# Half of the tokens of a PEER layer through all experts densely on TensorE, the other half still gathered

## The chip, the cores and the metric

The kernel runs on one core of a Trainium2 chip. The metric is the device time of one execution in microseconds, as the median of several runs; lower is better. A core has TensorE (PE, matmuls into PSUM, with weight loads listed as PEld), VectorE (DVE), ScalarE (ACT), GpSimd (POOL) and SyncE (SP), and 16 DMA engines that all queues share. SP issues plain transfers, POOL the indirect ones (gathers of rows by index).

## What is computed

One encoder layer over 512 tokens of width 1024, in float32: a token-mixing part (spatial gating and retention), then PEER, a retrieval over 16,384 experts that each are one row of `u` and one of `v`. Every token picks 16 experts in each of 8 heads:

```python
q = (h @ w_q).reshape(b, s, PEER_HEADS, 2, PEER_KEY_DIM)
scores = jnp.einsum('bshpd,hpnd->bshpn', q, sub_keys)     # 2 x 128 keys per head
top_s, top_i = lax.top_k(scores, 16)                      # of each half
cand_s = top_s[..., 0, :, None] + top_s[..., 1, None, :]  # 256 candidates
cand_i = top_i[..., 0, :, None] * 128 + top_i[..., 1, None, :]
best_s, best_pos = lax.top_k(cand_s.reshape(...), 16)
gates = softmax(best_s)                                   # over the 16
act = gelu(einsum('td,ted->te', x, u_tab[idx]))
out = einsum('te,ted->td', gates * act, v_tab[idx])
x <- LayerNorm(2**0.25 * h + out)
```

An expert's number is 128 i + j, from the two halves' keys i and j.

## The kernel before, in words

The tokens lie on the 128 partitions in four tiles (NT = 4). The token-mixing part runs first and is the same in both kernels up to the output projection ("out") and the first layer norm. For the rest, a *unit* is one head of one tile of tokens: 32 units of 16 experts for 128 tokens. For each unit and each of its 16 choices, POOL gathers 128 rows of `u` (one per token, 4 KB each, 512 KB in all) and later 128 rows of `v`, into rings of RING = 8 buffers each (`urow`, `vrow` in `big`). Every gather is one indirect DMA (L427, `block_of_gathers`), the two tables in turn.

- DVE, per unit (`unit`): 8 dot products of `u` rows with the tokens (`products`, L863, which also reads the sum out), the sum of an earlier unit out of PSUM (`add_unit`, L856), the choice of the *next* unit's experts (`choose`, L799 to L848: top 16 of 128 twice, top 16 of 256, indices), 8 more products, and the weights (L875).
- ACT, per unit: the exponentials, the GELU of the 16 dots, and 16 diagonal matrices of the weights (`diagonals`, L504).
- PE, per unit: `add_rows` (L1011), per expert two matmuls of 512 columns, diagonal matrix times the 128 `v` rows, that sum up in PSUM.
- Only the first units are written out, between the heads' queries (L969, `query`) and key scores (L1152, `keys`) on PE; from unit 8 (PE, ACT, DVE) or 2 (POOL) the engines run loops.

`static_jobs` writes the order of PE's and ACT's work by hand and gives each job its PSUM bank. One float32 matmul shows as two MATMUL records in the trace.

## Time and profile before

| | us |
|---|---|
| median of 3 runs | 1776.52 |
| lowest, highest run | 1762.88, 1776.70 |
| span of the profiled execution, first to last instruction | 1921.2 |
| PE busy in it | 1402.8 |
| DVE busy | 1125.5 |
| POOL busy | 1186.6 |

For the profiled execution only the span is known; what lies around its first and last instruction isn't in the page. Busy shares are means over the front part (about 244 us here) and the expert part, which have different limits. "issue" is the name for an engine's idle time in which it waited for nothing that the profile shows.

### The profile page before, as it was taken

Reading aid. Unit: us, or ns where it says so; the run is one execution under the profiler, and the core shown is the slowest. Engines: PE = TensorE matmul, PEld = TensorE weight load, DVE = VectorE, ACT = ScalarE, POOL = GpSimd, SP = SyncE. Lnnn points to the kernel's source line nnn. Section 1 sums busy time; section 2 is a strip of 40 time slices with the busy share of each in tenths; the row PEclk is TensorE's granted clock in tenths of the full one; section 3 lists DMA queues with packets and bytes.
Section 4 is the critical chain, followed back from the end, with each engine's and each line's share of the span. In section 5 each row is a group of like instructions: output and inputs, shape, how many; then the busy total and the mean of one; then the engine's idle time right before and its main releaser. Section 6 shows DMA issues by size and latency. Waiting matters only on the chain.

```text
span 1921.2 us, 14461 instructions
## 1 busy us (share of the span) xinstructions
PE 1402.8 (73%) x3572; PEld 633.5 (33%) x3572; DVE 1125.5 (59%) x2765; ACT 344.1 (18%) x792; POOL 1186.6 (62%) x1061
## 2 busy tenths in 40 slices
PE   8999798889899865566665666576657666675666
PEld 6777444334345322222222222122212222222222
DVE  5663578555655557555655655655546565546565
ACT  4230112222112211111111111111111111111110
POOL 2341177666676765677766666676767666667764
PEclk9999898999999998899988998898989889998989
DMA  6214299988999998788988889798979888888987
GB/s 230 84 71 148 91 354 332 383 323 324 343 360 341 357 347 299 289 322 326 340 318 307 317 334 353 261 368 314 357 277 355 304 307 318 310 334 310 367 294 264
DMA packets 173537, 577.87 MB, mean 301 GB/s; under 512 B 17712, under 2 KB 30512, under 8 KB 173488
## 3 DMA queue, kind: packets, MB, share of 16 engines
q0 software_dynamic: 147456, 536.94, 75.6%
q1 hardware_dynamic: 26032, 40.38, 6.0%
q8 instruction: 19, 0.31, 0.1%
q14 instruction: 30, 0.25, 0.0%
HBM read 575.15 MB, written 2.10 MB: 300 GB/s over the span
## 4 chain that ended last, share of the span: by engine, by line
PE 22%; DVE 20%; issue 20%; DMA 15%; POOL 14%; DVEq 6%; another core or an unknown queue 2%; ACT 1%; POOLq 0%; SPq 0%; ACTq 0%
POOL big L427 14%; DMA big<-in_peer_u_dram,idxu 11%; PE ps L1011 7%; DVE big L863 7%; PE ps L969 5%; PE ps L986 5%; DMA big<-in_peer_v_dram,idxv 4%; DVE y L856 1%; DVE mixT L802 1%; DVEq L818 1%; DVE topi L801 1%; DVE pick L846 1%; DVEq L800 1%; DVE top L804 1%
## 5 line engine op out<-in xcount | busy, mean ns | idle before, releaser
L1011 PE MATMUL ps<-big,diag 128*128 128x512 f32 x1968 | 1001.4, 644 | 472.6 <-DMA big<-in_peer_v_dram,idxv 219.5
L863 DVE CUSTOM_DVE_ANT_0 big<-big,mixT 128x1024 f32<-128x1024 f32 x480 | 571.6, 1224 | 417.0 <-DMA big<-in_peer_u_dram,idxu 399.9
L427 POOL DMA_INDIRECT big<-in_peer_v_dram,idxv x496 | 557.9, 1125 | 306.1 <-issue 145.0
L1011 PEld LDWEIGHTS ps<-big,diag 128*128 128x128 f32 x1968 | 364.6, 201 | 1100.9 <-issue 787.8
L427 POOL DMA_INDIRECT big<-in_peer_u_dram,idxu x512 | 548.0, 1070 | 264.3 <-issue 144.5
L504 ACT ACTIVATE diag<-ident,wgt 128x128 f32<-128x128 f32 x508 | 159.6, 389 | 500.0 <-PE ps L1011 370.3
L334 POOL TENSOR_TENSOR weight_parts<-big,weight_parts 128x1024 fp32r<-128x1024 f32 x20 | 49.0, 2474 | 84.6 <-ACT weight_parts L486 84.5
L969 PE MATMUL ps<-xT,qkT 128*128 128x512 f32 (+1 forms) x256 | 98.9, 539 | 1.1 <-ACTq L571 1.1
L986 PE MATMUL ps<-weight_parts,x_hi 128*128 128x512 f32 x320 | 82.8, 404 | 0.8 <-ACT weight_parts L486 0.8
L969 PEld LDWEIGHTS ps<-xT,qkT 128*128 128x128 f32 x256 | 48.6, 190 | 50.1 <-issue 35.3
L986 PEld LDWEIGHTS ps<-weight_parts,x_hi 128*128 128x128 f32 x320 | 59.8, 191 | 14.8 <-ACT weight_parts L486 2.4
L496 ACT ACTIVATE gel<-dots 128x16 f32<-128x16 f32 x32 | 6.9, 216 | 309.6 <-DVE dots L863 309.5
L490 ACT ACTIVATE eg<-best,negmax 128x16 f32<-128x16 f32 x33 | 10.1, 307 | 279.3 <-DVE negmax L832 192.6
L486 ACT ACTIVATE mixT<-ps 128x512 f32<-128x512 f32 (+1 forms) x20 | 11.1, 555 | 234.4 <-PE ps L969 118.1
L863 DVE DVE_READ_ACCUMULATOR2_ANT dots<- 128x1 f32 x512 | 41.9, 82 | 0.0
L490 ACT ACT_TABLE_LOAD x32 | 41.1, 1283 | 0.7
L496 ACT ACT_TABLE_LOAD x32 | 41.1, 1283 | 0.6
L986 PE MATMUL ps<-weight_parts,x_lo 128*128 128x512 f32 x160 | 40.2, 394 | 0.0
L863 DVE CUSTOM_DVE_ANT_0 big<-big,y 128x1024 f32<-128x1024 f32 x32 | 37.3, 1222 | 3.6 <-DMA big<-in_peer_u_dram,idxu 3.4
L856 DVE TENSOR_TENSOR y<-y,ps 128x1024 f32 (+1 forms) x32 | 38.9, 1216 | 0.2
L804 DVE MAX8 best<-mixT 128x8 f32<-128x256 f32 x30 | 12.8, 428 | 42.7 <-issue 41.6
L986 PEld LDWEIGHTS ps<-weight_parts,x_lo 128*128 128x128 f32 x160 | 30.6, 192 | 6.7
(179 smaller groups left out, 947.5 us busy)
## 6 DMA issues: line engine op xcount, KB each, us to landing
big<-in_w_in_dram SPq DMA_DIRECT2D x24, 512.0 KB, 5.8
qkT<-in_peer_w_q_dram SPq DMA_DIRECT2D x12, 1024.0 KB
big<-in_peer_u_dram,idxu POOLq DMA_INDIRECT x512
big<-in_peer_v_dram,idxv POOLq DMA_INDIRECT x496
xh<-in_x_dram SPq DMA_DIRECT2D x8, 512.0 KB, 10.7
big<-in_w_out_dram SPq DMA_DIRECT2D x2, 2048.0 KB, 10.7
out_dram<-y SPq DMA_DIRECT2D x8, 256.0 KB
lnp<-in_ln_w_dram SPq DMA_DIRECT2D x2, 512.0 KB, 6.9
```

The source lines that it names most:

```text
L334: return engine.tensor_tensor(w_lo(g)[:, ks, :], w_full(g)[:, ks, :], w_hi(g)[:, ks, :].bitcast(f32), ALU.subtract)
L427: nc.gpsimd.indirect_dma_start(row[e % RING], None, table, bass.IndirectOffsetOnAxis(ap=index[:, e:e + 1], axis=0)).then_inc(signal[e % RI ...
L490: A.activation(eg[:, k, :], best[:, k, :], ACT.Exp, bias=negmax[:, k:k + 1], accum_out=esum[:, k:k + 1]).then_inc(s_exp, 1)
L496: A.activation(gel[:, k, :], dots[:, k, :], ACT.Gelu).then_inc(s_gel, 1)
L504: A.activation(diag[:, e % NDIAG, :], ident[:], ACT.Copy, scale=wgt[:, k, e:e + 1]).then_inc(s_diag, 1)
L800: fence()
L804: V.max(values[:, 8:16], spare)
L856: V.tensor_tensor(yt, yt, acc[k], ALU.add).then_inc(s_yadd, 1)
L863: V.tensor_tensor_reduce(out=urow[e % RING], in0=urow[e % RING], in1=hcur, scale=1.0, scalar=0.0, op0=ALU.mult, op1=ALU.add, accum_out=dot ...
L969: last = T.matmul(dst, lhs(i), rhs(i), start=(i == 0), stop=(i == n - 1))
L986: last = T.matmul(dst, *((a, b_) if x_left else (b_, a)), start=(n == 0 and k == 0), stop=(n == 2 and k == KC - 1))
L1011: last = T.matmul(acc[k][:, half * 512:(half + 1) * 512], diag[:, e % NDIAG, :], ring[e % RING][:, half * 512:(half + 1) * 512], start=(e ...
```

## The change

Tiles 0 and 1 (GATHERED = 2; 16 units) stay gathered. Tiles 2 and 3 (DENSE = 256 tokens) go through all 16,384 experts:

- the host writes `u` a second time, as 128 blocks in a transposed layout (`u_blocks`); SP streams the 128 `u` blocks and the 128 `v` blocks of 128 experts, 512 KB each, through a ring of four buffers (`load_block`), in two rounds: 64 `u` blocks, 64 `v` blocks, twice.
- "act" on PE: per `u` block 8 matmuls of 256 columns, and ACT's GELU of two blocks at a time into `X` (128 experts x 256 tokens per block i).
- "gates": DVE builds for each token two one-hot matrices over its 128 choices, one of key j (128 wide) and one of key i (64 wide in a round) times the gate (`onehots`); PE multiplies them (64 columns per token), which gives the token's 128 x 64 gate matrix; DVE multiplies it into `X` (`dense_weights`). `gate_round` does 32 groups of 8 tokens per round.
- "expert" on PE: per `v` block 4 matmuls of 512 columns, weights `X`, into the PSUM banks that the gathered sums used.
- the gathered half no longer uses PE and the diagonals: DVE adds each gathered `v` row times its weight to the tokens' sum (`add_rows`, L897 of the changed kernel), two units behind the products.
- DVE chooses for the 16 dense heads of two tiles at a stroke, 5, 5 and 6 of them in the first three units. The gate rounds stand behind unit 3 and unit 11.
- all loops are written out; buffers are laid over one another in `pool_mem`; POOL takes a `u` row and a `v` row in turn, each waiting for one slot of its ring instead of four.
- queries of tiles 0/1 and 2/3 are separate matmuls, since the transposed tokens lie in two halves; the first chooses and the norms of tiles 1 to 3 change places.

```diff
+GATHERED = 2
+GUNITS = GATHERED * PH
+DENSE = (NT - GATHERED) * P
+HALF = NK // 2
+DRING = 4
+FILL = list(range(16, HALF)) + list(range(16))
...
+    for r in range(2):
+        for n in range(HALF // 2):
+            add("act", r, n, by="act")
+            for u in after.get((r, n), ()):
+                jobs.append(("gelu", (u,), None))
+        if r == 0:
+            jobs.append(("gates", (), None))
+            add("selT", 0, by="act")
+            add("selT", 1, by="act")
+        for n in range(DENSE // 8):
+            add("gate", r, n, by="dve")
+        for u in range(3, 8) if r == 0 else range(12, GUNITS):
+            jobs.append(("gelu", (u,), None))
+        for n in range(HALF):
+            jobs.append(("expert", (r, n), None))
...
+            def load_block(b):
+                r, n = divmod(b, 2 * HALF)
+                if b == 1:
+                    sp.wait_ge(s_sc0, TILE0)
+                elif b == 2:
+                    sp.wait_ge(s_wqd, TILE0 + PH)
+                elif b >= DRING:
+                    sp.wait_ge(s_blkd, b - DRING + 1)
...
+            def gather_u(n):
+                u, e = divmod(n, TOPK)
+                if e == 0:
+                    pool.wait_ge(s_idx, u + 1)
+                if n >= RING:
+                    pool.wait_ge(s_dot, n - RING + 1)
...
+            def gather_v(n):
+                if n >= RING:
+                    pool.wait_ge(s_vadd, n - RING + 1)
...
+            lag = 2 * TOPK
+            for n in range(GUNITS * TOPK + lag):
+                if n < GUNITS * TOPK:
+                    gather_u(n)
+                if n >= lag:
+                    gather_v(n - lag)
...
+            def add_rows(u, e0, e1):
+                for e in range(e0, e1):
+                    n = TOPK * u + e
+                    dve.wait_ge(s_v[n % RING], 16 * (1 + n // RING))
+                    V.scalar_tensor_tensor(acc_rows[t], vrow[n % RING], wgt[:, u, e:e + 1], acc_rows[t],
+                                           ALU.mult, ALU.add).then_inc(s_vadd, 1)
                     fence()
...
+                V.tensor_tensor(ohi[:, q], spread(0, HALF),
+                                iota[:, r * HALF:(r + 1) * HALF].unsqueeze(1).broadcast_to([P, 4, HALF]),
+                                ALU.is_equal)
+                V.tensor_tensor(ohj[:, q], spread(1, NK), iota[:].unsqueeze(1).broadcast_to([P, 4, NK]),
+                                ALU.is_equal)
+                fence()
+                V.tensor_tensor(ohi[:, q], ohi[:, q], spread(2, HALF), ALU.mult)
+                fence().then_inc(s_oh, 1)
...
+            chooses = [5, 5, 6]
+            for u in range(GUNITS):
+                products(u, 0, TOPK // 2)
+                if u >= 2:
+                    weights(u - 2)
+                    add_rows(u - 2, 0, TOPK // 2)
+                if u + 2 < GUNITS:
+                    choose_gathered(u + 2)
+                if u < len(chooses):
+                    for n in range(sum(chooses[:u]), sum(chooses[:u + 1])):
+                        choose_dense(n)
...
+                products(u, TOPK // 2, TOPK)
...
+                if u >= 2:
+                    add_rows(u - 2, TOPK // 2, TOPK)
+                if u == 3:
+                    gate_round(0)
+                if u == 11:
+                    gate_round(1)
...
+            for u in range(GUNITS - 2, GUNITS):
+                weights(u)
+                add_rows(u, 0, TOPK)
+            finish(acc_rows[1]).then_inc(s_ln2, 1)
             fence()
+            dve.wait_ge(s_vdone, 1)
+            for a in range(2):
...
+                rows_v = block_of(r, HALF + i)
+                for a in range(2):
+                    for half in range(2):
+                        last = T.matmul(acc[a][:, half * 512:(half + 1) * 512], X[:, i, a * P:(a + 1) * P],
+                                        rows_v[:, half * 512:(half + 1) * 512], start=(r == 0 and i == 0),
+                                        stop=(r == 1 and i == HALF - 1))
...
+                        last = product(bank[:, q * DENSE:(q + 1) * DENSE], lambda k: cols[:, k, :],
+                                       lambda k: hT[:, 1, k, :], KC)
+                        T.drain().then_inc(s_blkd, 1)
```

PE, behind the last norms of the first part. In the kernel before, queries (L969), key scores (L1152) and the expert rows of the first units (L1011, `S` and `big` hold the `v` rows, `diag` the diagonals) alternate:

```order
L1119 MATMUL ps<-ident,xh 128x128 x8
L969 MATMUL ps<-xT,qkT 128x512 x8
L1011 MATMUL ps<-big,diag 128x512 x10
L969 MATMUL ps<-xT,qkT 128x512 x8
L1152 MATMUL ps<-keysT,mixT 128x128 x8
L1011 MATMUL ps<-big,diag 128x512 x22
```

In the changed kernel the last query and keys are followed by the blocks, one row per ring buffer (`wr`, `y` and two in `xT`), with 256 columns a matmul, and, further on, by the transposes of the choices and the gate matmuls of the first round:

```order
L1012 MATMUL ps<-xT,pool_mem 128x256 x8
L1197 MATMUL ps<-pool_mem 128x128 x9
L1012 MATMUL ps<-xT,wr 128x256 x8
L1012 MATMUL ps<-xT,y 128x256 x8
L1012 MATMUL ps<-xT 128x256 x16
```

```order
L1209 MATMUL ps<-ident,sel 128x128
L1210 MATMUL ps<-ident,sel 128x128
L1211 MATMUL ps<-ident,gated 128x128
L1219 MATMUL ps<-ohi,y 128x64 x256
```

PE no longer has any row of a gathered unit; its whole expert part hangs on the blocks and on the one-hots.

DVE, the end of one unit and the start of the next. Before (unit 2 and 3; `ISA` is a product or its read-out):

```order
L863 ISA big,dots<-big,mixT 128x1024
L863 ISA dots 128x1
L872 RECIPROCAL rsum<-esum 128x1
L875 SCALAR_TENSOR_TENSOR wgt<-gel,rsum,eg 128x16
L863 ISA big,dots<-big,mixT 128x1024
L863 ISA dots 128x1
```

In the changed kernel, at unit 3's end, 8 rows are added (`y` is the sum), and the gate round follows, one group of 8 tokens being two sets of three rows and one product into `X` (in `pool_mem`):

```order
L877 ISA big,dots<-big,xh 128x1024
L877 ISA dots 128x1
L897 SCALAR_TENSOR_TENSOR y<-big,wgt,y 128x1024 x8
L914 TENSOR_TENSOR ohi<-selT,iota 128x256
L917 TENSOR_TENSOR y<-selT,iota 128x512
L920 TENSOR_TENSOR ohi<-ohi,selT 128x256
L914 TENSOR_TENSOR ohi<-selT,iota 128x256
L917 TENSOR_TENSOR y<-selT,iota 128x512
L920 TENSOR_TENSOR ohi<-ohi,selT 128x256
L927 TENSOR_TENSOR pool_mem<-ps,pool_mem 128x64x8
```

Every unit of the gathered half now has two such groups of 8 added rows on DVE, which PE did before.

## Rows read from the trace of the kernel before

**Rows 1.** The page: span, busy time, chain of waits, queue of gathers.
```profile
span 1921.2 us, 14461 instructions
PE 1402.8 (73%) x3572; PEld 633.5 (33%) x3572; DVE 1125.5 (59%) x2765; ACT 344.1 (18%) x792; POOL 1186.6 (62%) x1061
...
q0 software_dynamic: 147456, 536.94, 75.6%
...
PE 22%; DVE 20%; issue 20%; DMA 15%; POOL 14%; DVEq 6%; another core or an unknown queue 2%; ACT 1%; POOLq 0%; SPq 0%; ACTq 0%
```

**Rows 2.** Groups by line and shape: busy us, mean ns | idle before, by releaser.
```profile
L1011 PE MATMUL ps<-big,diag 128*128 128x512 f32 x1968 | 1001.4, 644 | 472.6 <-DMA big<-in_peer_v_dram,idxv 219.5 <-ACT diag L504 212.0 <-issue 40.9
L863 DVE CUSTOM_DVE_ANT_0 big<-big,mixT 128x1024 f32<-128x1024 f32 x480 | 571.6, 1224 | 417.0 <-DMA big<-in_peer_u_dram,idxu 399.9 <-issue 16.1
L427 POOL DMA_INDIRECT big<-in_peer_v_dram,idxv x496 | 557.9, 1125 | 306.1 <-issue 145.0 <-PE ps L1011 96.8 <-DVE idxu L848 42.0
...
L804 DVE MAX8 best<-mixT 128x8 f32<-128x256 f32 x30 | 12.8, 428 | 42.7 <-issue 41.6
...
L834 DVE CAST posf<-posab 128x32 f32<-128x32 uint32 x33 | 6.4, 193 | 25.9 <-issue 23.9
...
L743 DVE TENSOR_TENSOR S<-ps,S 128x512 f32<-128x512 f32 x4 | 2.7, 685 | 0.1
```

**Rows 3.** Stretches of 5 us: busy per engine, PEclk, DMA share, GB/s.
```profile
330.00:335.00 5.00, 5.00 (x15) 2.19 (x14) 5.00 (x10) 0.00 (x0) 4.39 (x3) 1.00 1.03 413
1030.00:1035.00 5.00, 3.83 (x9) 1.25 (x8) 1.23 (x6) 0.00 (x0) 3.78 (x5) 1.00 1.04 416
1040.00:1045.00 5.00, 1.92 (x4) 0.61 (x4) 4.64 (x10) 0.00 (x0) 1.33 (x1) 1.00 0.18 30
1045.00:1050.00 5.00, 0.00 (x0) 0.00 (x0) 5.00 (x9) 0.00 (x0) 2.84 (x2) 0.66 0.44 143
```

**Rows 4.** PE in order of time: start us, us, line, shape, records.
```profile
217.23 5.35 PE L1127 MATMUL ps<-xT,qkT 128*128 128x128 f32 x32
...
259.43 3.73 PE L1127 MATMUL ps<-xT,qkT 128*128 128x128 f32 x32
...
264.43 13.90 PE L969 MATMUL ps<-big,mixT 128*128 128x512 f32 x32
...
352.94 7.03 PE L969 MATMUL ps<-xT,qkT 128*128 128x512 f32 x16
```

**Rows 5.** DVE in order of time, one choose and the first products.
```profile
234.41 0.28 DVE L799 MAX8 top<-ropet 128x8 f32<-128x128 f32 x1
...
244.46 1.23 DVE L863 CUSTOM_DVE_ANT_0 big<-big,y 128x1024 f32<-128x1024 f32 x1
245.61 0.08 DVE L863 DVE_READ_ACCUMULATOR2_ANT dots<- 128x1 f32 x1
245.61 1.22 DVE L863 CUSTOM_DVE_ANT_0 big<-big,y 128x1024 f32<-128x1024 f32 x1
```

**Rows 6.** POOL in order of time; DVE's products run back to back until 268.3.
```profile
262.57 1.99 POOL L427 DMA_INDIRECT big<-in_peer_u_dram,idxu  x1 [0.30 <-issue]
...
269.45 0.94 POOL L427 DMA_INDIRECT S<-in_peer_v_dram,idxv  x1 [0.30 <-issue]
```

**Rows 7.** DVE in order of time: pairs of 256 elements, an added row, a norm.
```profile
231.62 0.76 DVE L839 TENSOR_TENSOR y<-posf,iota 128x256 f32<-128x256 f32 x2
232.45 0.76 DVE L844 TENSOR_TENSOR y<-y,topf 128x256 f32<-128x256 f32 x2
...
1910.29 1.28 DVE L957 SCALAR_TENSOR_TENSOR y<-big,wgt,y 128x1024 f32<-128x1024 f32 x1
1911.65 1.29 DVE L645 BATCH_NORM_STATS2 st<-y 128x6 f32<-128x512 f32 x2
...
1917.95 0.75 DVE L653 SCALAR_TENSOR_TENSOR y<-y,nw,lnp 128x512 f32<-128x512 f32 x1
```

**Rows 8.** The page's DMA issues: transfer, queue, count, KB each, us to landing.
```profile
big<-in_w_in_dram SPq DMA_DIRECT2D x24, 512.0 KB, 5.8
```

More of the change, by code:

```diff
@@ L147, in static_jobs @@
     for i, (kind, arg, by) in enumerate(jobs):
-        if kind in ("V", "split", "norm"):
+        if kind in ("split", "norm", "scale", "gelu", "gates", "expert"):
             placed.append((kind, arg, by, None, None))
@@ L499, in diagonals @@
-            def diagonals(u, k, e0=0, e1=TOPK, first=False):
-                for e in range(e0, e1):
-                    if (e % 4 == 0 or e == e0) and not (first and e < NDIAG):
-                        act.wait_ge(s_vexp, 16 * u + min(e - e % 4 + 4, e1) - NDIAG)
-                    A.activation(diag[:, e % NDIAG, :], ident[:], ACT.Copy,
-                                 scale=wgt[:, k, e:e + 1]).then_inc(s_diag, 1)
-            act.wait_ge(s_const, 4)
-            A.activation(gel[:, 0, 0:1], ident[:, 0:1], ACT.Gelu)
@@ L592, in _ @@
                     A.drain().then_inc(s_sc, 1)
[L594 to L604 removed]
+                elif kind == "act":
+                    r, n_ = arg
+                    i = FILL[2 * n_] if r == 0 else 2 * n_
+                    if i == 0 and r == 0:
+                        act.wait_ge(s_chosen, 2 * PH)
+                    if i == 48 and r == 0:
+                        act.wait_ge(s_h, 2 * NT)
+                    A.activation(X[:, i:i + 2, :], bank.rearrange("p (i n) -> p i n", i=2), ACT.Gelu
+                                 ).then_inc(free[b], 1)
+                    if n_ == HALF // 2 - 1:
+                        A.drain().then_inc(s_act, 1)
+                elif kind == "selT":
+                    a = arg[0]
+                    copy(selT[:, :, a * P:(a + 1) * P], bank4[:, 0:3, :]).then_inc(free[b], 1)
+                    A.drain().then_inc(s_selT, 1)
+            for t in range(GATHERED):
+                for half in range(2):
+                    act.wait_ge(s_ln2, 2 * t + half + 1)
+                    c = half * 512
+                    act.dma_start(out3[:, t, c:c + 512], acc_rows[t][:, c:c + 512]).then_inc(s_out, 16)
         @block.vector
@@ L827, in choose @@
                 fence()
[L828 removed]
+                top16(cand, values, pos[:], spare)
                 fence()
@@ new lines, in dense_weights, with gate_round @@
+            def dense_weights(r, n):
+                b, used_ = BANK["gate", r, n]
+                dve.wait_ge(full[b], used_ + 1)
+                x3 = X[:, :, 8 * n:8 * n + 8]
+                V.tensor_tensor(x3, ps[:, b, :].rearrange("p (t i) -> p i t", t=8), x3, ALU.mult).then_inc(free[b], 1)
+            def gate_round(r):
+                if r == 0:
+                    dve.wait_ge(s_selT, 2)
+                for n in range(DENSE // 8):
+                    onehots(r, n, 0)
+                    onehots(r, n, 1)
+                    if n == 1:
+                        dve.wait_ge(s_act, r + 1)
+                    if n:
+                        dense_weights(r, n - 1)
+                dense_weights(r, DENSE // 8 - 1)
+                fence().then_inc(s_wgtd, 1)
@@ L1162, in _ @@
                     T.drain().then_inc(s_scored, 1)
-            for u in range(EARLY, PH):
-                add_rows(u, u % 2)
-            with pe.Fori(PH // 2, UNITS // 2 - 1) as pair:
-                add_rows(2 * pair, 0)
-                add_rows(2 * pair + 1, 1)
-            add_rows(UNITS - 2, 0)
-            add_rows(UNITS - 1, 1, 0, LAST, end=LAST)
+            T.drain().then_inc(s_vdone, 1)
 _INS = ["x", "w_in", "sgu_ln_w", "sgu_ln_b", "sgu_w_s", "sgu_b", "ret_decay_fwd", "ret_decay_bwd", "ret_gn_w",
```

484 lines of the change are left out of this document (228 added, 256 removed).

## The prediction

> **What bounds the kernel now.** I read the page first: PE is busy 73% of 1921.2 us, POOL 62%, DVE 59%, and the chain of waits is spread over PE, DVE, POOL, DMA and "issue" with 14 to 22% each [rows 1]. No engine is the bound alone; a loop through several is. The groups by line say which: DVE's products sit idle 399.9 us for the gathered `u` rows, PE's expert rows 219.5 us for the `v` rows [rows 2]. So I looked at the transfers by stretch. While POOL issues without a pause they carry 413 to 416 GB/s at a share of 1.03 to 1.04; once per unit the rate falls to 30 and 143 GB/s, when DVE's choose had made POOL wait [rows 3]. POOL takes 0.94 + 0.30 = 1.24 us per gather [rows 6], and 0.524 MB per 1.24 us is 423 GB/s. The kernel before lives on this stream: 536.9 MB of gathers [rows 1], which alone need 1309 us at 410 GB/s.
>
> The profiled execution takes 1921.2 us and the runs 1776.5 us, 145 us less. DVE's choose shows idle time put down to "issue", 41.6 and 23.9 us in two of its groups alone [rows 2], and none where transfers are light: the choose at 234.41 runs through in 10.05 us [rows 5]. I take such gaps as the profiler's and work with durations without them. My sum is thus for a run without a profiler; set against the profiled execution's own 1921.2 us I would add about 60 to 110 us (22 of the 32 chooses under heavy transfers, at 3 to 5 us), giving a span of 1830 to 1880 for the changed kernel. A forecast made only in ratio to the span (1855 / 1921) would be 1715 us; I keep it inside the range.
>
> **The change part by part.** Removed: 16 of 32 units' gathers (268.4 MB), all diagonals, all L1011 matmuls. Added: 256 blocks of 0.524 MB (134.2 MB) from SP. Transfers of the expert part fall to 268.4 + 134.2 + 8.4 (the query weights) = 411 MB, 1002 us at 410 GB/s. That is room, if it can be used evenly.
>
> *PE.* 32 records of 512 columns take 13.90 us, 0.434 each; 32 of 128 columns 3.73 us, 0.117 each [rows 4]. An expert block is 8 records of 512: 3.47 us. An act block is 16 records of 256 columns: between 16 x 0.117 = 1.9 and 16 x 0.434 = 6.9 us; the two rows lie on a line through 0.22, so 3.5 us, and 0.1 for the drain. 128 blocks of each: 890 us. Queries: eight heads at 2 x 7.03 us, four of them three quarters of that, 98 us, and 112 records of 128 columns for the keys, 13 to 19 us at 0.117 to 0.167, in all some 115 us [rows 4]; they begin when tile 3 is normed.
>
> *DVE.* A product costs 245.61 - 244.46 = 1.15 us [rows 5]; 256 of them 294 us. An added row costs 1911.65 - 1910.29 = 1.36 us [rows 7]; 256: 348 us, which is new on DVE. Chooses: 32 x 10 = 320 us, as before. A gate group of 8 tokens: a pair of 256 elements with its fence takes 0.83 us [rows 7] and 512 elements from PSUM 0.685 us [rows 2], so 256 + 512 + fence 1.1, the second 256 0.5, twice, + 0.7 = 3.9 us; with hand-overs to PE 4.1. Lower bound 3.5 (all fences free), upper bound 3.9 + 8 x 2 x 0.167 = 6.6 (PE's records at the pace of its slower row, 5.35 us for 32 [rows 4], with nothing overlapped; the two sets of one-hot buffers speak for the low end). 32 groups: 131 us a round, and in it neither gathers nor blocks move but for full rings: this is the cost with nothing beside it, 262 us in two rounds.
>
> *The rings.* POOL's `v` gather needs a slot that only an added row frees. In the 8 products (9.2 us) it is stuck; then it owes DVE 16 gathers, 16 x 1.24 = 20 us, against 8 x 1.36 us of adding. Where DVE computes back to back, a gather takes up to 1.99 instead of 0.94 us [rows 6]; I add half of that, 0.5 us.
>
> The path, by stage:
> 1. To the start of the units: the last out group of tile 3 ends at 264.43 + 13.90 = 278.3 [rows 4]; two residuals and the norm (1911.65 to 1918.7, 7.1 us [rows 7]) take it to 287, choose(1) to 298.
> 2. Units 0 to 3: 64 products 73, 32 added rows 44, 4 chooses 40 and 16 dense ones at 9.8, 157, small ones 4: 317. Rows come late by some 5, 7, 12 and 12 us in the halves without a choose (20 us of POOL against 20 of DVE with a landing behind it): 353. This ends at 651. PE ends its queries at about 289 + 115 = 404 and the first 64 act blocks at 632, so it is hidden.
> 3. Gate round 0: 131, to 782.
> 4. Units 4 to 11. PE runs 64 expert and 64 act blocks, 450 us. DVE needs 16 x 1.15 + 16 x 1.36 + 10 + 1 = 51 us a unit. But PE's blocks take 0.524 MB per 3.5 us, 150 GB/s, and leave 260 of 410 for the gathers: 16.78 MB a unit is 64.5 us, plus 4 in which POOL is stuck, 69 us. Eight units: 6.5 in PE's 450 us, 1.5 at 51 + 4 to 5: 530; by bytes alone, 201 MB at 410, 491. I take 526, to 1308.
> 5. Gate round 1: 131, to 1439.
> 6. Units 12 to 15: 64 expert blocks, 222 us of PE; 3.2 units at 69 and 0.8 at 43, one norm 8: 255. Then 32 added rows, 44, plus 6 of waits, norm 8: 313, to 1752. PE is done at 1439 + 222 = 1661, hidden.
> 7. Two residuals and norms, 2 x 8.7, and the last store 2.5: 1772 us.
>
> Against 1776.5 that is no change. What halving the gathers gives, the gate rounds (262 us) and DVE's added rows (348 us) take back.
>
> The critical price is stage 4's rate. Of this the trace shows only one queue at a time at full load; two queues may carry less (370, which is 536.94 MB over 75.6% of the span [rows 1]) or more. At 370 the stages that hang on transfers give 1848, at 430 some 1735. I take 410, by the nearest rows. The Trainium skill (DMA: Bandwidth & Descriptors, "Where 436 GB/s comes from") puts the limit for loads from HBM at about 358 GB/s and the ports' at 435. The trace's 416 is above the first; by the second the sum would be an estimated 1727.
>
> **The rivals.**
> - *The stream hides it all* (faster). If the transfers of blocks and gathers don't hold each other up, stage 4 is PE's 450 and stage 6 DVE's 240 + 10: 1772 - 76 - 63 gives about 1635. For it: DVE and PE have slack in every stage. Against: it asks for 150 + 16.78 MB / 53 us = 467 GB/s, and no stretch shows over 416 [rows 3].
> - *The added rows lock POOL out* (slower). One mechanism: POOL's gather waits while DVE runs an op with two SBUF operands. Products show it: 1.99 us against 0.94, a pace of one gather per two products [rows 6]. Now all of the `v` slots come free during such ops. At a full 1.05 us more per gather issued in them, 16 gathers a unit lose 0.55 more each, 9 us, of which half is behind the stream: 4 to 5 us x 10 units in stages 2, 4, 6 adds about 45: 1818. It decides from about 0.8 us. Against: over the whole trace the mean gather is 1.125 [rows 2], so most slip between. The Trainium skill (SBUF — State Buffer, "SBUF: two separate sides") says a DVE op with two SBUF inputs and a GpSimd op that reads SBUF exclude each other for the whole instruction. It speaks against moving these sums from PE to DVE; rows 6 agree for products, and no run here shows it for an added row with its fence.
> - *PE is the bound of the gate rounds.* PE is busy half of the time there; if its clock falls to 1.2 GHz (the granted 0.66 of one stretch stands where PE was idle [rows 3]) and half of its work lies bare, a group takes 3.9 + 1.35 = 5.25 us, 37 more a round: 1846. It decides once PE's half group is longer than DVE's 1.6 us.
> - *The change doesn't do what it says*: blocks starve PE since the ring is four deep. 3 x 3.5 = 10.5 us of lead against a landing of 5.8 us for 512 KB [rows 8]; unlikely, and inside the last case.
>
> **How the numbers follow.** The forecast, 1772 with its own range 1735 to 1810, has a chance of 0.5; the hidden stream 0.2 (1635, with cases up to 1735); the lock 0.24 (1800 to 1840); the gate rounds on PE or starving 0.06 (1846). Within 1% of 1776.5 is 1759 to 1794, about what a measurement of this kernel can tell from no change. Of the forecast's half, 0.18 lies under, 0.20 within, 0.12 above. Faster by over 1%: 0.18 + 0.20 = 0.38, with 0.02 from the reading in ratio to the span 0.40; same 0.22; slower 0.12 + 0.24 + 0.06 less rounding, 0.38. The range for 8 in 10 reaches to 370 GB/s above and halfway to the hidden stream below: 1685 to 1850.
>
> **What would show it.** In the changed profile: act blocks in 3.5 us and expert blocks in 3.47; units 4 to 7 at 65 to 73 us with 390 GB/s or more and DVE's products and added rows waiting for gathers; gate rounds of 125 to 140 us with hardly a transfer; PE idle before gate round 1; the last PE matmul some 80 us before the end. Wrong would be: units 4 to 7 at 55 us (hidden stream), gathers of nearly 2 us in the added rows (lock), gate rounds over 150 us, or a span under 1780.

## The result and the profile after

The changed kernel takes 1868.06 us (median of 4 runs, 1864.51 to 1877.42) against 1772.6 us (4 runs) beside it: a ratio of 1.057, interval 1.052 to 1.063. It is 5.7% slower. On other occasions the kernel before itself takes 1917 to 1936 us (experiment 8), and the ratio there is 0.979. The forecast was 1772 in a range of 1685 to 1850, so the time lies 96 us over the forecast and 18 us outside the range.

The page of the changed kernel, against [rows 1]:

```profile
span 1862.6 us, 17614 instructions
...
PE 1535.9 (82%) x5898; PEld 1096.9 (59%) x5898; DVE 1305.2 (70%) x2763; ACT 170.5 (9%) x268; POOL 634.9 (34%) x548
...
PE   8999899999999805999999979789728999999500
...
DVE  5663367877683179888586576686688888755688
...
PEclk9999999999999955558999989899865559999855
DMA  6223334375954385006999989899983009999883
...
q0 software_dynamic: 73728, 268.47, 37.8%
```

POOL's busy time fell from 62% to 34% of the span and the gathers' bytes to half, as forecast. The time went into what the rows of digits show as holes. DVE falls to 1 and PE to 0 just ahead of the first gate round (slices 13 to 15); the transfers stand at 0 in both rounds; and PE's clock stands at 5 in both.

The span by the stages of the prediction, one stretch each (busy us per engine in the order PE, PEld, DVE, ACT, POOL, then PE's granted clock, the transfers' share and GB/s):

```profile
298.00:718.00 420.00, 335.00 (x1587) 276.44 (x1585) 277.94 (x839) 53.68 (x90) 103.68 (x92) 0.91 0.61 213
718.00:845.00 127.00, 116.69 (x512) 111.61 (x512) 111.96 (x224) 0.00 (x0) 9.23 (x9) 0.50 0.13 48
845.00:1397.00 552.00, 468.13 (x1537) 293.36 (x1536) 387.88 (x688) 42.67 (x72) 271.75 (x246) 0.93 0.92 355
1397.00:1527.00 130.00, 117.81 (x513) 112.18 (x514) 114.94 (x227) 0.00 (x0) 10.31 (x10) 0.50 0.13 51
1527.00:1841.00 314.00, 221.21 (x512) 97.49 (x510) 228.96 (x340) 9.77 (x16) 163.67 (x144) 0.85 0.90 343
```

| stage | forecast | measured |
|---|---|---|
| 2: units 0 to 3 | 353 | 420 |
| 3: gate round 0 | 131 | 127 |
| 4: units 4 to 11 | 526 | 552 |
| 5: gate round 1 | 131 | 130 |
| 6: units 12 to 15, last rows, norm | 313 | 314 |

Stages 2 and 4 are 67 + 26 = 93 us over, against 96 in all. The other three are right within 4 us.

Stage 2 is told by one row. DVE's waits, the two longest groups, and DVE and ACT in order of time around the second:

```profile
DVE big L877 <- DMA big<-in_peer_u_dram,idx: 242.9, 100, 5.1
DVE dsum L864 <- ACT gated L511: 69.2, 1, 69.2
```

```profile
576.01 1.22 DVE L877 CUSTOM_DVE_ANT_0 big<-big,xh 128x1024 f32<-128x1024 f32 x1
577.16 0.08 DVE L877 DVE_READ_ACCUMULATOR2_ANT dots<- 128x1 f32 x1
646.49 0.42 DVE L864 TENSOR_REDUCE dsum<-gated 128x16 f32<-128x256 f32 x1 [69.25 <-ACT gated L511]
```

```profile
636.30 0.60 ACT L587 ACTIVATE pool_mem<-ps 128x512 f32<-128x512 f32 x1 [7.15 <-PE ps L1012]
644.05 0.60 ACT L587 ACTIVATE pool_mem<-ps 128x512 f32<-128x512 f32 x1 [7.15 <-PE ps L1012]
644.74 1.28 ACT L511 ACT_TABLE_LOAD   x1
646.04 0.42 ACT L511 ACTIVATE gated<-gated 128x256 f32<-128x256 f32 x1
```

DVE has everything for the dense gates at 577 and needs one exponential of ACT. ACT is idle 7.15 us ahead of nearly every eviction (an eviction is the GELU that takes a pair of act blocks out of PSUM), but it works in the order of its program, and there the exponential (L511) stands behind the evictions of all 64 act blocks of round 0. So DVE waits for PE's whole act pass by way of ACT. Behind DVE's wait, on DVE, are the added rows of unit 2's second half and all of unit 3, none of which need a gate of the dense half.

### The profile page after: what moved, and what is told of

It is laid out like the page before. It is cut to its first block, busy times and chain, and to the rows that moved or that the text cites. A ratio compares the mean times of both kernels' runs of the same rounds, so it can differ in the third digit from the quotient of the medians.

```text
span 1862.6 us, 17614 instructions
## 1 busy us (share of the span) xinstructions
PE 1535.9 (82%) x5898; PEld 1096.9 (59%) x5898; DVE 1305.2 (70%) x2763; ACT 170.5 (9%) x268; POOL 634.9 (34%) x548
## 4 chain that ended last, share of the span: by engine, by line
PE 29%; DVE 23%; POOL 17%; DMA 16%; issue 8%; DVEq 5%; ACT 1%; SPq 0%; ACTq 0%
PE ps L1012 19%; DMA big<-in_peer_u_dram,idx 16%; POOL big L471 10%; POOL big L461 7%; DVE y L897 6%; PE ps L1029 5%; DVE big L877 3%; DVEq L919 3%; DVE ohi L920 3%; DVE pool_mem L927 2%; DVE y L917 2%; DVE ohi L914 1%; PE ps L1219 1%; PE ps L1197 1%; PE ps L1151 1%
## 5 line engine op out<-in xcount | busy, mean ns | idle before, releaser
L877 DVE CUSTOM_DVE_ANT_0 big<-big,xh 128x1024 f32<-128x1024 f32 x256 | 303.9, 1223 | 247.5 <-DMA big<-in_peer_u_dram,idx 242.9
L461 POOL DMA_INDIRECT big<-in_peer_u_dram,idx x256 | 275.8, 1077 | 587.2 <-DVE dots L877 457.5
L471 POOL DMA_INDIRECT big<-in_peer_v_dram,idx x256 | 298.1, 1164 | 466.2 <-DVE y L897 396.7
L897 DVE SCALAR_TENSOR_TENSOR y<-big,wgt,y 128x1024 f32<-128x1024 f32 x256 | 328.7, 1284 | 22.8 <-issue 1.0
L1219 PE MATMUL ps<-ohi,y 128*128 128x64 f32 x1024 | 233.6, 423 | 122.9 <-DVEq L921 122.9
L1219 PEld LDWEIGHTS ps<-ohi,y 128*128 128x128 f32 x1024 | 223.3, 330 | 133.7 <-issue 133.5
L1012 PE MATMUL ps<-xT 128*128 128x256 f32 x1024 | 243.5, 392 | 36.8 <-ACT pool_mem L587 26.7
L1012 PEld LDWEIGHTS ps<-xT 128*128 128x128 f32 x1024 | 193.8, 194 | 86.5 <-issue 33.6
L1064 PE MATMUL ps<-xT,pool_mem 128*128 128x512 f32 x512 | 224.9, 592 | 0.0
L1064 PEld LDWEIGHTS ps<-xT,pool_mem 128*128 128x128 f32 x512 | 97.3, 190 | 122.5 <-issue 122.5
L1012 PEld LDWEIGHTS ps<-xT,pool_mem 128*128 128x128 f32 x512 | 87.3, 193 | 12.1 <-issue 2.5
```

The source lines that it names most:

```text
L461: nc.gpsimd.indirect_dma_start(urow[n % RING], None, peer_u2, bass.IndirectOffsetOnAxis(ap=idx[:, u, e:e + 1], axis=0)).then_inc(s_u[n % R ...
L471: nc.gpsimd.indirect_dma_start(vrow[n % RING], None, peer_v2, bass.IndirectOffsetOnAxis(ap=idx[:, u, e:e + 1], axis=0)).then_inc(s_v[n % R ...
L877: V.tensor_tensor_reduce(out=urow[n % RING], in0=urow[n % RING], in1=xh[:, t * D:(t + 1) * D], scale=1.0, scalar=0.0, op0=ALU.mult, op1=AL ...
L897: V.scalar_tensor_tensor(acc_rows[t], vrow[n % RING], wgt[:, u, e:e + 1], acc_rows[t], ALU.mult, ALU.add).then_inc(s_vadd, 1)
L1012: last = T.matmul(dst, lhs(i), rhs(i), start=(i == 0), stop=(i == n - 1))
L1064: last = T.matmul(acc[a][:, half * 512:(half + 1) * 512], X[:, i, a * P:(a + 1) * P], rows_v[:, half * 512:(half + 1) * 512], start=(r == ...
```

## The experiments

All medians are of runs on a chip beside runs of the kernel before. The changed kernel itself took 1868, 1871 and 1875 us on three occasions, so differences of up to 7 us between runs on different chips are not read. Experiments 1 to 4 ran beside a slower level of the kernel before, which experiment 8 takes up.

**1. The exponential earlier on ACT.**

```diff
-        if r == 0:
-            jobs.append(("gates", (), None))
+            if (r, n) == (0, 22):
+                jobs.append(("gates", (), None))
```

> ACT takes the exponential of the dense gates after act block pair 22 of round 0 (some 575 us) instead of after pair 31 and its table load (646 us). Theory A (the 69.2 us in which DVE waits for this exponential lie on the path, and nothing behind takes them back): DVE's idle time ahead of dsum goes from 69 to under 8 us, gate round 0 begins near 655 instead of 718, every later stage keeps its length, and the time falls by 60 to 67 us, to about 1803. Rival B (the pause is only where DVE waits for PE's act blocks, which gate round 0 needs anyway): the act pass ends at 644 or later, since unit 3's gathers now run beside it, the wait moves to the first product of gates and act blocks, and 20 us at most are won: 1848 or more. Rival C (the wait let the transfers get ahead): the 60 us are won in stage 2 and half of them is lost in stage 4: about 1835.

Measured: 1813.78 us, 54 less than the first runs of the changed kernel. Gate round 0 begins at 667.0, 51 us sooner, and the stages behind it take 130, 546, 128 and 319 us, in all what they took before. DVE's wait ahead of the sums:

```profile
587.38 0.42 DVE L865 TENSOR_REDUCE dsum<-gated 128x16 f32<-128x256 f32 x1 [8.67 <-ACT gated L512]
```

Theory A holds, with 54 us where it said 60 to 67 and 8.67 us of wait left where it said under 8. Not all of the 60 us come back: between the sums and the round DVE now waits 11.1 us for gathers, up to 3.1 for one, instead of 8.0, and once 4.5 us for nothing that the profile shows. Nothing behind takes any of it back, and rivals B and C fall. Against the changed kernel of run 8, which ran beside the same slower level, gate round 0 begins 62 us sooner (729.1 there) and the time is 61 less.

**2. The same wait moved on DVE instead.**

```diff
-                if u == len(chooses) - 1:
-                    dense_gates()
                 if u == 3:
+                    dense_gates()
                     gate_round(0)
```

> DVE takes the dense gates (its wait for ACT's exponential with them) after unit 3's last added row, directly ahead of gate round 0; ACT's order stays. Theory A: DVE does the added rows and products of units 2 and 3 while ACT works through the act blocks; the exponential ends at about 650, DVE comes to it at about 650 as well, then the sums, PE's two transposes and ACT's copies (some 4 us) lie bare, so gate round 0 begins near 660 and the time falls by 55 to 62 us, to about 1808: nearly the same as with the exponential moved on ACT, which would show that the order of the two engines and not either's load is the cause. Rivals B and C as for the exponential taken early: 1848 or more, 1835.

Measured: 1817.53 us. DVE now waits 21.7 us for the exponential, after unit 3, where none was forecast; in the profile, of the slowest of the four runs (1824.15), gate round 0 begins at 680.0 and not near 660. Both orders win the same within 4 us: it is the pair of orders, not the load of either engine, that made the 69 us.

**3. No gate rounds.** The one-hot rows, the gate matmuls and the product of gates and act blocks are left out (in `gate_round` only the waits for ACT and the fence at its end stay, and the "gate" jobs go).

> Both gate rounds are left out: no one-hot rows, no gate matmuls, no product of gates and act blocks (the expert matmuls take the act blocks without gates); all the rest stays, DVE's wait for the exponential of 69 us too. Theory (DVE's gate work is on the path for all of its 127 + 130 us, since neither gathers nor block loads go on in it): the time falls by 240 to 257 us, to 1611 to 1628. Rival (the rounds also let rings fill and PE get ahead, so that part of the 257 comes back as waits for rows): it falls by 190 to 220, to 1650 or more.

Measured: 1643.28 us, 225 less than the first runs of the changed kernel and 232 less than its 1875 in run 8. That lies between the two expectations. DVE's wait for the exponential is 84.2 us here, 69.2 in the first profile of the changed kernel and 79.5 in that of run 8, so 5 to 15 us of what is missing to 257 are this. What the gate rounds cost in the time is 225 to 247 us, against 262 forecast.

**4. Block loads of an eighth.** From the fifth block on a load brings 64 KB instead of 512 KB; what PE multiplies by is then mostly stale.

```diff
-                sp.dma_start(dring[b % DRING], src).then_inc(s_blk[b % DRING], 16)
+                dst = dring[b % DRING]
+                if b >= DRING:
+                    dst, src = dst[:, 0:P], src[:, 0, :] if n < HALF else src[:, 0:P]
+                sp.dma_start(dst, src).then_inc(s_blk[b % DRING], 16)
```

> Each block load after the first four brings 64 KB instead of 512 KB (an eighth of the columns; PE multiplies by what else stands in the ring), so 252 of the 256 loads lose 0.46 MB each, 116 MB of 444; the gathers, PE's and DVE's work stay. Theory D (in units 4 to 11 gathers and block loads share a stream of 410 GB/s and that sets the pace): these units go from 550 to PE's or ACT's bound, 64 expert and 64 act blocks at 3.43 and 3.87 = 467 us, or 8 x 53 = 424 if PE isn't it; units 12 to 15 win 30 to 45 more; the time falls by 100 to 130 us, to 1740 to 1768. Rival E (the gathers' own pace of POOL, 1.37 beside added rows and 1.24 otherwise, and the ring of eight bind, block loads cost nothing): less than 30 us, 1840 or more.

Measured: 1787.39 us, 81 to 88 less. Theory D in kind, under its 100 to 130 in size. A unit takes 60 to 62 us instead of 72, and DVE comes to gate round 1 after 476 us instead of 552. There it waits for PE, whose act pass ends 501 us after the stage's start:

```profile
DVE big L880 <- DMA big<-in_peer_u_dram,idx: 118.5, 70, 4.2
...
DVE ohi L917 <- PE ps L1222: 24.3, 4, 22.7
```

The loads cost 12 us a unit. The forecast had 16 (69 against 53), because it took 53 for a unit without them and 60 was measured; DVE still waits 57.5 us for gathers in this stage. PE, taken for 450 us in it, is the bound at 501.

**5. Half of the drains.**

```diff
-                        T.drain().then_inc(s_blkd, 1)
+                        if q == 0:
+                            last.then_inc(s_blkd, 1)
+                        else:
+                            T.drain().then_inc(s_blkd, 1)
```

> Of PE's 128 drains behind the act blocks the 64 behind the first block of a pair go (the last matmul of that block frees the ring's buffer itself). A pair takes 7.75 us in the changed kernel's profile against 2 x 3.5 of the forecast. Theory H (a drain costs 0.25 us of PE): 16 us less in act pass 0, which the exponential of the gates and so gate round 0 follow: gate round 0 begins at 710 instead of 718; the drains of act pass 1 are hidden, since gathers set that stage's pace; the time falls by 6 to 10 us, to about 1860. Rival (the 0.37 us over the forecast lie in the matmuls themselves and in waits for blocks): no change within 3 us.

Measured: 1865.36 us, 10 less than the changed kernel on the same chip; gate round 0 begins at 718.9 there against 729.1. Theory H in kind (of the 64 drains only 32 are in act pass 0, so its 16 us were for both passes): 10 us for 32 drains, some 0.3 us each where the forecast had 0.1. ACT's evictions show the same without a comparison of starts, one every 7.41 us instead of every 7.75, 0.34 us for the drain that is gone:

```profile
562.90 0.60 ACT L587 ACTIVATE pool_mem<-ps 128x512 f32<-128x512 f32 x1 [6.81 <-PE ps L1012]
570.31 0.60 ACT L587 ACTIVATE pool_mem<-ps 128x512 f32<-128x512 f32 x1 [6.81 <-PE ps L1012]
```

They show in the time because the exponential hangs on act pass 0. The 729.1 itself is 11 us later than in the first profile of the changed kernel; experiment 8 says what is known of that.

**6. A unit inside each gate round.** With the early exponential; unit 4 and unit 12 are cut into steps of one product or one added row, and one step goes behind each group of 8 tokens.

```diff
                     if n:
                         dense_weights(r, n - 1)
+                    next(steps, lambda: None)()
...
-                products(u, 0, TOPK // 2)
+                if u in (4, 12):
+                    gate_round(u // 12, unit_steps(u))
```

> The exponential taken early, and unit 4 (8 products, 8 added rows, choose and so on, one step behind each group of 8 tokens) goes into gate round 0, unit 12 into gate round 1. Theory I (gate rounds cost DVE time while transfers stand still, and the stages behind them are bound by transfers at 69 us a unit): each round grows by 51 us to some 180, and the stage behind it loses one unit, 69 us: 18 us each, 36 in all, 1814 - 36 = 1778. Rival J (PE's 64 expert and 64 act blocks, 467 us, take over as the bound of the middle stage as soon as it has seven units): the first 18 are won only as 10, in all 20 to 28: 1786 to 1794.

Measured: 1806.15 us, only 8 less than with the early exponential alone, and these two ran on different chips. The rival's mechanism, and stronger than it said. DVE gets through the middle stage's seven units in 488 us instead of 546 for eight, but PE needs 506, and DVE waits for it at the head of gate round 1:

```profile
DVE ohi L915 <- PE ps L1235: 15.8, 1, 15.8
```

**7. The gates multiplied on ACT.** As 6, and ACT, idle in the rounds, scales the one-hot rows.

```diff
-                V.tensor_tensor(ohi[:, q], ohi[:, q], spread(2, HALF), ALU.mult)
...
+                            A.activation(ohi[:, q, j, :], ohi[:, q, j, :], ACT.Copy, scale=selT[:, 2, t:t + 1])
```

> As the kernel with a unit in each round, and besides ACT multiplies the one-hot rows by the gates (four scaled copies of 64 columns per half group) instead of DVE. DVE loses 128 x (0.425 + 0.1) = 67 us. Theory K (with a unit inside, DVE is the bound of both rounds, 5.5 us a group, and PE with 3.65 isn't): both rounds fall from 180 to about 148 us, the time by 55 to 67 us, to 1712 to 1722 if the kernel with a unit in each round takes 1778. Rival L (DVE to ACT to PE to DVE is now a chain with two buffers, ACT's four copies at some 0.2 us and its hand-over with it: a group can't be under 2 x (0.5 + 1.0 + 1.8) = 6.6 us): the rounds grow by 30 us each and the time to about 1840.

Measured: 1778.26 us, 28 less than 6. Half of the theory's gain: the first round takes 157 us instead of 173 (the theory had 148), but DVE now waits for PE in it, and 27.7 us at the head of the second round:

```profile
DVE ohi L924 <- PE ps L1242: 59.3, 63, 27.7
```

**8. The changed kernel again, on two more occasions.** The kernel before had shown a median of 1936 us beside experiments 1 to 4, so the base itself was in question.

> The changed kernel, unaltered, once more, beside runs of the kernel before on the same chip, since the first runs of this study found the kernel before at a median of 1936 us where it had 1773 us beside the changed kernel. Theory F (the kernel before has two levels, 1770 and 1920 to 1940, which go with the chip or its memory, and the changed kernel doesn't): 1868 again within 1%, beside about 1935 of before, so that the ratio is 0.965 here. Rival G (the chip of these runs is slower for both): the changed kernel takes 2030 us, 8 to 9% more, and the exponential taken early (1814) has won 220 us.

> The changed kernel, unaltered, beside these, so that they are compared on one chip. Theory F (only the kernel before has two levels): 1865 to 1875, whichever level the kernel before shows beside it. Rival G: 8% more where the kernel before is at its slower level.

> The kernel before, unaltered, for a profile on the same chip. Theory F: a span like the profiled execution's 1921 us, with idle time put down to issue in the chooses (41.6 us ahead of L804's best, 23.9 ahead of posf): these gaps are then no work of the profiler but part of the slower level of this kernel. Rival: a span near its runs of 1770 and no gaps.

> The kernel before, unaltered, with a profile. Theory F: the gaps put down to issue in DVE's chooses go with this kernel's slower level: where this chip runs it at 1905 to 1940 us, the profile has some 200 us of them, as the profile that the prediction was read from; where it runs at 1760 to 1780, under 30 us, as the second profile. Rival: gaps and level are independent.

Measured: the changed kernel 1870.53 beside 1772.47 of the kernel before (1.057), and 1874.96 beside 1917.04 (0.979). In the times theory F holds: only the kernel before has two levels. Its two new profiles are both of the faster one, 1768.4 and 1756.1 us, and neither has the gaps in the chooses. One of the two groups of [rows 2], in the profile of 1768.4 us:

```profile
L804 DVE MAX8 best<-mixT 128x8 f32<-128x256 f32 x30 | 12.8, 428 | 2.2
```

The idle time ahead of this group was 42.7 us in the profile at 1921.2. Over all of DVE's groups that are listed, the idle time put down to issue is 209 us at 1921.2, 19 at 1768.4 and 18 at 1756.1. The last profile and experiment 9, beside which the kernel before took 1926 us, carry the same chip number a few minutes apart, so the level may belong to the occasion and not to the chip. What causes it stays open, since no run of these caught a profile of the kernel before at the slower one.

The profiles of the changed kernel do show a difference that its times hide. PE's idle time put down to issue ahead of the act blocks and the queries, in the first profile and in that of run 8:

```profile
PE ps L1012 <- issue: 15.6, 60, 0.3
PE ps L1012 <- issue: 43.6, 65, 7.2
```

The first row is the short pause behind each drain and nothing else, and so it is in the profile beside 1772.47. Beside the slower level PE also stands still for 2 to 7 us at a time: act pass 0 takes 258 us instead of 248, and gate round 0 begins at 729.1. Every profile of experiments 1 to 7, of 9 and of the first run of 10 has such pauses, and each of these ran beside the slower level.

**9. ACT's gelus of units 8 to 11 later.** With the early exponential; they stand behind pairs 15 and 24 and the last instead of 6, 14, 22 and 30.

> The exponential taken early, and ACT's four gelus of round 1, of units 8 to 11, stand behind act block pairs 15 and 24 and behind the last one instead of 6, 14, 22 and 30. In the kernel with the early exponential alone PE's matmuls of act pass 1 sit idle some 40 us while ACT waits for DVE's dots with PE's evictions behind the wait. Theory M (this order is what takes the middle stage of 8 units from 516 us, 201 MB at the 390 GB/s that its first 75 us reach, to 546): PE's idle time there falls under 10 us, act pass 1 ends near 1290 instead of 1320, the block loads come sooner, the stage takes 520 to 530 us and the time is 1790 to 1800. Rival N (the gathers' stream alone sets the stage, PE's pauses lie beside it): act pass 1 ends 30 us sooner, DVE reaches gate round 1 no sooner, and the time stays within 5 us of 1814.

Measured: 1813.48 us, no change, and the middle stage is 547 us again. But the run doesn't decide between the two, since its edit did not do what both of them ask: PE's act pass ends at 1314 instead of 1316, not 30 us sooner. Of PE's idle time in that pass 40.2 us were put down to issue and 2.1 to ACT with the early exponential alone, and 29.1 and 16.9 are now, so most of it was no wait for ACT. The second run of experiment 10 has the shorter pass.

**10. All five edits together**, in two runs.

> All together: exponential early, one unit in each gate round, gates multiplied on ACT, half of the drains, ACT's gelus of units 8 to 11 later. In the kernel with the first three (1778 us) PE's act pass 1 ends at 1340 and DVE waits for it with its first product of gate round 1, although the gathers are ahead. Theory M': without ACT's waits the middle stage of seven units is 483 us by PE (64 x 3.43 + 64 x 3.87 = 467, less 16 by the drains) or by transfers instead of 514, so the time is 1745 to 1755, below the faster level of the kernel before (1772). Rival N': the middle stage stays at 505 or more, and the time at 1770 to 1780.

> The kernel with all five edits again, beside the kernel before on this chip. Theory: 1755 to 1762 whatever the chip; against the kernel before that is 0.993 where that one is at its faster level (1772) and 0.915 where it is at its slower one (1925). Rival: this kernel too has a faster level, some 5% lower, on chips where the kernel before has it, then 1680.

Measured: 1760.04 us beside 1925.86 (0.916) and 1763.22 beside 1771.4, the ratio 0.9957 with an interval of 0.9935 to 0.9979. DVE's seven units take 485 us, as in 6 and 7 (488 and 483), but PE's part of the stage ends after 492 us instead of 506 and 511, so that DVE's longest wait for it falls from 27.7 to 15.1 us. That is the first run. Its time lies between the 1745 to 1755 of theory M' and the 1770 to 1780 of rival N'. The second run's misses its 1755 to 1762 by 1 us, and its rival, 1680, falls. Gate round 0 with its unit, and the middle stage, against the stretches of the changed kernel above:

```profile
660.00:815.00 155.00, 116.71 (x512) 111.62 (x512) 130.23 (x245) 70.28 (x260) 39.93 (x37) 0.50 0.40 131
815.00:1300.00 485.00, 451.90 (x1503) 289.79 (x1504) 342.63 (x605) 38.02 (x62) 246.42 (x219) 0.97 0.97 371
```

The second run has no pauses in PE's act pass and ends at nearly the same time by another path. The middle stage in its profile, and DVE's waits for PE:

```profile
812.00:1316.00 504.00, 450.69 (x1536) 289.83 (x1536) 343.45 (x605) 44.74 (x73) 240.48 (x220) 0.96 0.94 363
...
DVE ohi L926 <- PE ps L1247: 31.0, 58, 0.7
```

PE is through with the stage after 461 us, 31 sooner than in the first run, DVE's seven units take 504 instead of 485, and gate round 1, in which DVE now waits at most 0.7 us for PE, takes 155 instead of 169. So a PE that is through sooner gained nothing in this stage, which is what rival N of experiment 9 says. It is no clean test of it, since the kernel before beside the two runs is at different levels, and why the units take longer here wasn't tested.

The scheme beats the kernel before by 0.4% at that kernel's faster level, which is next to nothing, and by 8% at its slower one. It takes 105 to 115 us of repairs to get there.

## Why the prediction was wrong, step by step

**Stage 2, the step that failed.** "PE ends its queries at about 289 + 115 = 404 and the first 64 act blocks at 632, so it is hidden." The first half is right: the act blocks begin at 396.4 and end at 644. The conclusion isn't. I compared the ends of two engines and didn't ask what DVE takes from ACT in between and where that stands in ACT's program. The exponential of the gates stands behind the last eviction, so stage 2 could not end before 644 plus 24 added rows, 16 products and a choose, whatever DVE's own sum of 353 gave. Experiments 1 and 2 show it by taking most of the wait away in two ways: 54 and 51 us. It was a wait that the change adds on DVE, and it has no term in the sum. DVE's own sum was a little short as well: with the early exponential the stage takes 369 us, of which 8.67 are what is left of the wait.

**Act blocks, a term too small.** 3.5 + 0.1 was forecast; a pair takes 7.75 us, 3.87 each (the 890 us for 128 blocks of each kind left the 0.1 out). A block's 8 matmuls, 16 records, run in 3.7:

```profile
396.38 3.62 PE L1012 MATMUL ps<-xT,wr 128*128 128x256 f32 x16
400.08 3.72 PE L1012 MATMUL ps<-xT,y 128*128 128x256 f32 x16
404.06 7.49 PE L1012 MATMUL ps<-xT 128*128 128x256 f32 x32 [0.26 <-issue]
```

The line through the rows of 128 and 512 columns gave 0.22 us a record, the rows here 0.23; the drain costs the rest (experiment 5). Over 64 blocks that is 248 us instead of 228 to 230. Act pass 0 began at 396 instead of 404 and still ended at 644 instead of 632, and those 12 us are all wait on DVE. In stage 4 it took PE from 450 to 468 us busy.

**Expert blocks and gate groups.** An expert block of 8 records takes 3.43 to 3.60 us (forecast 3.47), a gate group 127 / 32 = 3.97 (forecast 4.1). Both right.

**Stage 4, a term too small by 26.** The units' sum was 530, of which I took 526. Forecast were 69 us a unit beside PE's blocks. The end of the chooses of units 5 and 6:

```profile
949.32 0.15 DVE L847 TENSOR_SCALAR negmax<-best 128x1 f32<-128x1 f32 x1
...
1022.00 0.15 DVE L847 TENSOR_SCALAR negmax<-best 128x1 f32<-128x1 f32 x1
```

72.7 us; over seven units the mean is 71.7. The rate that I doubted is right: two queues together reach 416 GB/s, as one queue does in [rows 3]. The holes are there too, two a unit:

```profile
925.00:930.00 5.00, 5.00 (x13) 2.23 (x12) 3.00 (x6) 0.00 (x0) 0.00 (x0) 1.00 1.02 397
930.00:935.00 5.00, 5.00 (x13) 2.27 (x12) 4.72 (x4) 0.00 (x0) 4.08 (x4) 1.00 0.71 251
945.00:950.00 5.00, 5.00 (x13) 2.25 (x12) 4.30 (x14) 0.00 (x0) 3.78 (x5) 1.00 1.03 416
```

```profile
930.00 1.92 POOL L471 DMA_INDIRECT big<-in_peer_v_dram,idx  x1 [13.69 <-DVE y L897]
932.23 1.07 POOL L461 DMA_INDIRECT big<-in_peer_u_dram,idx  x1 [0.30 <-issue]
933.60 1.06 POOL L471 DMA_INDIRECT big<-in_peer_v_dram,idx  x1 [0.30 <-issue]
```

POOL stands 13.7 us at a `v` gather whose buffer comes free only with the next added row. The rings' backlog covers most of it and then runs out: 5 us at 251 instead of 410 GB/s lose 1.9 us of stream, the 2 us that I gave a half unit. What I may have got wrong is its price. I wrote 64.5 + 4. If PE's blocks take their 150 GB/s all the time, lost stream is made up at 260: 4 us cost an estimated 4 x 410 / 260 = 6.3, and the unit 70.8 of the 71.7 measured. The other part would be PE. I let it be through after 450 us, with 1.5 units left to run at 55. It ends after 519: 468 busy, 39 in waits for ACT, the rest in small gaps. That left 0.8 of a unit for the faster pace.

```profile
PE ps L1012 <- ACT pool_mem L587: 39.0, 4, 12.7
```

Both parts are worked out and not shown. The second run of experiment 10 speaks against them: there PE is through after 461 us, an act block comes every 3.70 us, by which a unit would be 69, and the units beside act blocks take 72 to 76. Shown is that the block loads cost 12 us a unit (experiment 4); how the rest of the 26 us splits stays open.

Stage 4 moves its bytes at a mean of 355 GB/s. The Trainium skill (DMA: Bandwidth & Descriptors, "Where 436 GB/s comes from") gives about 358 GB/s for loads from HBM, as one core's half of what two share. The mean lies near that by chance: stretches of 5 us reach 416, so 358 was no limit here, and the stage's first 25 us at 214 GB/s, the holes and PE's waits bring the mean down.

**The rivals.** *The stream hides it all* didn't come. Even with loads of an eighth (experiment 4) a unit takes 60 us, and PE bounds the stage at 501. *The added rows lock POOL out*: the mechanism came, and the price was too high. All 110 gathers of stage 4 that begin within an added row end 0.81 or 0.82 us after that row does, so each waits for the row's end. The added rows beside the gathers above are these:

```profile
928.45 10.92 DVE L897 SCALAR_TENSOR_TENSOR y<-big,wgt,y 128x1024 f32<-128x1024 f32 x8
```

They take 1.28 us each and follow one another every 1.38, so the third runs until 932.48, and the gather that began at 932.23 ends at 933.30. The Trainium skill (SBUF — State Buffer, "SBUF: two separate sides") has the two exclude each other for a whole instruction. For the added row's side these rows agree. For the gather's they don't: the next added row begins at 932.58, with the gather still running. The lock is cheap because one gather with its pause, 1.24 us, fits into an added row's 1.38: the gathers fall into the rows' pace and each takes 1.07 us instead of 0.94. Only the first after a wait, two a unit, begins near a row's start and takes 1.92. That is 14 x 0.13 + 2 x 0.98 = 3.8 us a unit where I priced 9, and about half of each hole of 1.9 us in the stream is that first gather's 0.98. *PE bounds the gate rounds*: the clock did fall, to 0.50 throughout, but a group took 3.97 us and not 5.25, because PE's 3.82 us for the two halves stay just under DVE's own work. The threshold that I named, PE's half group over DVE's 1.6 us, was wrong: PE's 1.91 us for a half are over it, and DVE's longest wait for PE in the rounds was 1.4 us; with two sets of buffers the whole groups compare. In experiments 7 and 10, where DVE does less, DVE does wait for PE.

**Stage 6, right by a slip.** 3.2 units at 69 and 0.8 at 43 are 255 without the norm's 8 that the recorded sum names beside them. With it the stage is 321 and the whole 1780, against 314 measured for the stage.

**The base.** "I take such gaps as the profiler's." They weren't. The profile I worked from was of the slower level of the kernel before, in a span of 1921.2 us, and the runs beside experiments 1 to 7, 9 and the first of 10 show that level as well (medians of 1917 to 1936). The durations were not touched by it, so no stage of the sum was. But it gave a margin that doesn't exist: I expected 60 to 110 us between the changed kernel's span and its runs, and there are 2. My span of 1830 to 1880 holds the 1862.6 measured, for a wrong reason, and the runs follow the span.

**Where the halved gathers went.** 268 MB less to gather, at the 410 GB/s of the forecast 655 us of stream. Half of that comes back as 134 MB of block loads. The rest went into 257 us of gate rounds with next to no transfers, and into the 420 us of stage 2, in which DVE has twenty chooses to do and transfers are at 0.61. Without the one wait the change (1814, experiment 1) is still 2% over the faster level of the kernel before, and 6% under the slower one that it ran beside.

## What to carry to other kernels

When a step waits for another engine, look for where the answer stands in that engine's program, and what stands ahead of it. An engine that is idle 90% of its time can still hold an instruction back for 69 us. "Hidden" is to be checked per hand-over and not by comparing where two engines end.

Stages that use one resource each in turn (here DVE in the gate rounds, transfers between them) gain from being laid over one another, but each repair shows only when the next bound has moved as well: the unit inside the round won 8 us alone, the gates on ACT 28 more, and the last two edits 15 to 18. Two profiles of the same kernel can divide such a gain differently between two stages (485 + 169 and 504 + 155 us in experiment 10), so read the sum of the two and not one of them.

If a profiled span and the timed runs differ by 8%, measure the base again before explaining the difference. And before a theory is called refuted by an unchanged time, look whether the edit changed what it was meant to change (experiment 9).

## What the runs showed of the hardware that I had not expected

- The kernel before has two levels, 1754 to 1783 and 1905 to 1978 us, with 18 to 19 and 209 us of DVE's idle time put down to issue, 177 of the 209 in the chooses' short instructions. The changed kernel ran 1865 to 1881 beside either, but with PE pauses of 2 to 7 us beside the slower one alone.
- PE's granted clock stayed at 0.50, the 1.2 GHz level, through both gate rounds of 127 and 130 us, in which PE was busy 92 and 91% with matmuls of 64 columns; in the changed kernel it had been idle 70.8 us before the first. The clock was 0.88 over the first 25 us of expert matmuls of 512 columns and 1.00 after. In the first run of experiment 10, with PE idle only 10.5 us ahead of the round, it was 0.50 again.
- A PE drain behind a block of 3.7 us costs 0.34 us (experiment 5).
- A gather's issue on POOL that begins within an added row of DVE (1.28 us, every 1.38) ends 0.81 or 0.82 us after that row: 1.07 us in step with the rows, 1.92 when it begins near a row's start, 0.94 with neither rows nor products beside it.
